# A decoder layer on one core: the first gate and up products in seven block products instead of eight

## The reference

```python
def swiglu(x, w_gate, w_up, w_down):
    return (jax.nn.silu(x @ w_gate) * (x @ w_up)) @ w_down
...
    x = x + 0.5 * swiglu(rmsnorm(x, ffn1_norm), ffn1_w_gate, ffn1_w_up, ffn1_w_down)
    h = rmsnorm(x, mix_norm)
    ...
    x = x + merged @ w_out
    x = x + 0.5 * swiglu(rmsnorm(x, ffn2_norm), ffn2_w_gate, ffn2_w_up, ffn2_w_down)
```

## Time and profile before

| | us |
|---|---|
| median of 3 runs (1655.89 to 1656.66) | 1655.98 |
| the profiled execution | 1656.42 |
| its span, first to last instruction | 1654.6 |
| TensorE busy in the span | 1609.5 |
| VectorE busy | 891.4 |
| ScalarE busy | 627.8 |

### The profile page before, as it was taken

The page is one execution under the profiler, slowest core; times in us unless marked ns, Lnnn a source line. Parts: engine busy times, 40 slices in busy tenths (PEclk is TensorE's granted clock), DMA queues, the critical chain, the costliest instruction groups (busy, mean ns, idle before and its releaser), DMA issues.

```text
span 1654.6 us, 30254 instructions
## 1 busy us (share of the span) xinstructions
PE 1609.5 (97%) x12544; PEld 1526.1 (92%) x12544; DVE 891.4 (54%) x1410; ACT 627.8 (38%) x993; POOL 4.5 (0%) x20
## 2 busy tenths in 40 slices
PE   7999999999999989999999999999999999999997
...
GB/s 128 92 80 89 89 77 93 97 82 85 68 114 56 126 269 71 64 82 84 103 91 100 92 125 102 109 224 92 87 88 90 98 103 96 99 93 105 85 79 67
DMA packets 246808, 164.34 MB, mean 99 GB/s; under 512 B 8350, under 2 KB 229779, under 8 KB 246714
## 3 DMA queue, kind: packets, MB, share of 16 engines
q1 hardware_dynamic: 246424, 162.46, 33.6%
...
q10 hardware_dynamic: 290, 0.57, 0.1%
...
## 4 chain that ended last, share of the span: by engine, by line
PE 88%; DVE 5%; ACT 2%; DMA 2%; issue 1%; SPq 1%; DVEq 0%; ACTq 0%
PE ps L444 57%; PE ps L1602 12%; PE ps L906 3%; PE ps L1125 2%; PE ps L1089 1%; PE ps L1325 1%; PE ps L1276 1%; PE ps L987 1%; PE ps L1395 1%; PE ps L427 1%; DVE small L2751 1%; PE ps L1174 1%; PE ps L1699 1%; PE ps L1439 1%; PE ps L1514 1%
## 5 line engine op out<-in xcount | busy, mean ns | idle before, releaser
L444 PE MATMUL ps<-xn_hi,w_hi 128*128 128x280 f32 (+1 forms) x1520 | 441.5, 290 | 3.6 <-DVE w_lo L415 2.9
L444 PE MATMUL ps<-xn_hi,w_lo 128*128 128x280 f32 (+1 forms) x1520 | 442.9, 291 | 0.0
L444 PE MATMUL ps<-xn_lo,w_hi 128*128 128x280 f32 (+1 forms) x1520 | 441.3, 290 | 0.0
L411 ACT ACTIVATE w_hi<-raw 128x1024 fp32r<-128x1024 f32 (+1 forms) x154 | 173.3, 1126 | 615.2 <-PE ps L444 602.8
L415 DVE TENSOR_TENSOR w_lo<-raw,w_hi 128x1024 fp32r<-128x1024 f32 (+1 forms) x154 | 201.3, 1308 | 181.9 <-ACT w_hi L411 181.7
L444 PEld LDWEIGHTS ps<-xn_hi,w_hi 128*128 128x128 f32 x1520 | 286.9, 189 | 4.5 <-DVE w_lo L415 3.1
L444 PEld LDWEIGHTS ps<-xn_hi,w_lo 128*128 128x128 f32 x1520 | 286.8, 189 | 0.0
L444 PEld LDWEIGHTS ps<-xn_lo,w_hi 128*128 128x128 f32 x1520 | 286.1, 188 | 0.0
L444 PE MATMUL ps<-h_hi,w_hi 128*128 128x280 f32 (+1 forms) x616 | 179.0, 291 | 0.0
L444 PE MATMUL ps<-h_hi,w_lo 128*128 128x280 f32 (+1 forms) x616 | 178.7, 290 | 0.0
L444 PE MATMUL ps<-h_lo,w_hi 128*128 128x280 f32 (+1 forms) x616 | 178.0, 289 | 0.0
...
## 6 DMA issues: line engine op xcount, KB each, us to landing
...
```

The lines of the kernel that those rows point to most:

```text
L411: act.activation(w_hi[s][:, 0:p.nk, :], raw[s][:, 0:p.nk, :], ACT.Copy).then_inc(hi_done[s], 1)
L444: mm = pe.matmul(ps[:, bank + half, 0:p.half], w[s][:, k, :], x[:, i, cols], start=first and k == 0 and a == 0, stop=last and k == p.nk - ...
```

## The change

The first gate and up stage becomes seven products as the second one is, at 280 columns. The functions of the second stage get the parameters `p` and `turn` (0 for the first, 1 for the second) and serve both; hardware loops of the first stage, and of the first down stage on TensorE, are written out. The blocks of the tokens are made as the tiles come from the transposes, pair by pair, with two buffers of `W4` and `T4` in the first stage; the token rows `xtok` and the buffers move to other places in memory. The sums of squares of the token rows move behind the blocks on ScalarE, and the row norm comes in panel 2, with bank 3 for that panel's first product. At the start the up panel is loaded ahead of the second half of the tokens. The first stage ends as the second does: all 22 tiles of h are rounded at the end, and `down_first` begins the down projection. In the second stage the rest of G of panel 1 moves ahead of the first gate sum. Semaphores are shared differently. The core of the diff, on SyncE, TensorE, ScalarE and VectorE in this order:

```diff
+        def a_bank(turn, j):
+            return 3 if turn == 0 and j == 2 else 4 * (j % 2)
...
+            def raw_gate(p, turn, j):
+                if j >= 1:
+                    after(sp, lo7, SPLIT7, turn, "g", j - 1)
...
-            load(sp, up1, 0, 0)
+            raw_gate(up1, 0, 0)
             load_x(0)
+            raw_up(up1, 0, 0)
             load_x(1)
-            load(sp, up1, 0, 1)
             sp.dma_start(con[:, 128:C_N], const_ap[:, 128:C_N]).then_inc(in_c, 16)
...
-            stream(up1, 1)
+            raw_panels(up1, 0)
             stream(down1)
...
-            def down(p, u):
-                down_tile(p, u, 0, 0, tiles=tile_lo)
-                down_tile(p, u, 0, 1)
...
+                down_first(p, u, 0)
+                for i in range(1, p.n):
+                    down_tile(p, u, i // 2, i % 2, at=place)
...
+            def seventh(p, w_of, block, bank, pairs=range(DT // 2), first=False):
+                for k in pairs:
+                    for a, (w, x) in enumerate(((0, XH), (0, XL), (1, XH))):
+                        mm = pe.matmul(ps[:, bank, 0:p.half], w_of(w)[:, k], x[:, k, block, 0:p.half],
+                                       start=first and k == 0 and a == 0, stop=k == DT // 2 - 1 and a == 2,
+                                       skip_group_check=True)
+                return mm
...
+            def fourth(p, turn, j):
+                after(pe, lo7, SPLIT7, turn, "u", j)
+                after(pe, part7, PART7, turn, "r3", j)
+                seventh(p, a22(j % 2), 5, a_bank(turn, j)).then_inc(product7, 1)
+            def third(p, turn, j):
+                after(pe, hidden7, HIDDEN7, turn, "u2", j)
+                seventh(p, s4(j % 2), 1, 4 * (j % 2) + 1).then_inc(product7, 1)
+            def sixth(p, turn, j):
+                after(pe, lo7, SPLIT7, turn, "s2", j)
+                after(pe, part7, PART7, turn, "r1", j)
+                seventh(p, s2, 6, a_bank(turn, j)).then_inc(product7, 1)
+            def seventh_last(p, turn, j):
+                after(pe, part7, PART7, turn, "r2", j)
+                seventh(p, s3, 4, a_bank(turn, j)).then_inc(product7, 1)
+            def strassen(p, turn):
+                if turn:
+                    after(pe, lo7, SPLIT7, turn, "g", 0)
+                    for k in range(DT // 2 - 1):
+                        token(turn, "l3", k)
+                        early_12(p, k)
+                    after(pe, lo7, SPLIT7, turn, "s31", 0)
+                    for k in range(DT // 2 - 1):
+                        token(turn, "lt", k)
+                        seventh(p, s1, 3, 1, (k,), first=True)
+                end_12(p, turn)
+                token(turn, "lq", DT // 2 - 1)
+                sixth(p, turn, 0)
+                if turn:
+                    norm(2, p, (3, 7))
+                seventh_last(p, turn, 0)
+                for j in range(1, FT):
+                    c = 4 * (j % 2)
+                    if j == 2 and turn == 0:
+                        row_norm()
+                    after(pe, lo7, SPLIT7, turn, "g", j)
+                    if j >= 2 and a_bank(turn, j) == c:
+                        after(pe, hidden7, HIDDEN7, turn, "h1", j - 2)
+                    seventh(p, a11, 0, a_bank(turn, j), first=True).then_inc(product7, 1)
+                    if j >= 2:
+                        after(pe, gate7, GATE7, turn, "g1", j - 2)
+                    if j == 2 and turn == 0:
+                        pe.wait_ge(rn_ready, 1)
+                    seventh(p, a12, 2, c + 2, first=True).then_inc(product7, 1)
+                    fourth(p, turn, j - 1)
+                    after(pe, lo7, SPLIT7, turn, "s31", j)
+                    if j >= 2:
+                        after(pe, gate7, GATE7, turn, "g2", j - 2)
+                    seventh(p, s1, 3, c + 1, first=True)
+                    sixth(p, turn, j)
+                    third(p, turn, j - 1)
+                    seventh_last(p, turn, j)
+                fourth(p, turn, FT - 1)
+                third(p, turn, FT - 1)
...
-            for i in range(DT + 1):
+            for i in range(DT):
                 keep_warm(IDLE.get(i, 0))
-                for s, ks in EARLY.get(i, ()):
-                    first_product(pe, up1, 0, s, ks)
-                if i == DT:
-                    break
                 for c in range(2):
                     if 128 * i == X_CHUNKS[c][0]:
                         pe.wait_ge(in_x[c], 16 * 5)
@@ -1039,28 +1192,34 @@
                     mm = transpose(ps[:, 4 + 2 * (i % 2) + c0 // 512, c0 % 512:c0 % 512 + 112],
                                    xtok[:, t, 128 * i:128 * i + 128], 112)
                 mm.then_inc(xt_full, 1)
+                if i == DT - 3:
+                    after(pe, lo7, SPLIT7, 0, "g", 0)
+                    token(0, "l3", 0)
+                    early_12(up1, 0)
+            token(0, "l3", 1)
+            early_12(up1, 1)
+            after(pe, lo7, SPLIT7, 0, "s31", 0)
+            for k in range(2):
+                token(0, "lt", k)
+                seventh(up1, s1, 3, 1, (k,), first=True)
+            early_12(up1, 2)
+            token(0, "lt", 2)
+            seventh(up1, s1, 3, 1, (2,), first=True)
             x_done(pe, DT - 2)
             x_done(pe, DT - 1)
-            pe.wait_ge(dg_ready, 1)
-            for t in range(5):
-                c0 = 64 + 112 * t
-                mm = pe.matmul(ps[:, 4 + c0 // 512, c0 % 512:c0 % 512 + 112], ones[0:112, :], dg[:, t, :],
-                               start=True, stop=True)
-            mm.then_inc(nm_full, 1)
-            first_product(pe, up1, 0, 1, [DT - 2, DT - 1])
-            up(up1)
+            strassen(up1, 0)
             down(down1, up1)
...
+            g_split(0, 0)
             act.wait_ge(ring_dve, 1)
             x_copy(1)
-            hi(0)
-            hi(1)
+            scaled_first(0)
+            scaled_first(1)
+            blocks_hi(up1, 0, 0)
             x_copy(3)
-            hi(2)
-            hi(3)
-            square_rows(0)
-            hi(4)
-            split_hi(act, up1, 0, 1)
-            hi(5)
-            square_rows(1)
-            square_rows(2)
-            hi(6)
-            hi(7)
+            scaled_first(2)
+            scaled_first(3)
+            differences_hi(up1, 0, 0)
+            blocks_hi(up1, 0, 1)
+            x_copy(5)
+            scaled_first(4)
+            scaled_first(5)
+            s31_split(0, 0)
+            differences_hi(up1, 0, 1)
+            x_copy(6)
+            blocks_hi(up1, 0, 2)
+            x_copy(7)
+            scaled_first(6)
+            scaled_first(7)
+            differences_hi(up1, 0, 2)
+            blocks_hi(up1, 0, 3)
+            differences_hi(up1, 0, 3)
+            s2_split(0, 0)
+            u_split(0, 0)
+            for t in range(3):
+                square_rows(t)
+            first_sum(up1, 0, 0)
+            g_split(0, 1)
             square_rows(3)
+            second_sum(up1, 0, 0)
+            s2_split(0, 1)
             square_rows(4)
+            u_split(0, 1)
+            third_sum(up1, 0, 0)
+            s31_split(0, 1)
+            first_sum(up1, 0, 1)
             act.wait_ge(in_c, 16)
             act.wait_ge(ss_ready, 5)
-            act.activation(r0[:, 0:5], r0[:, 0:5], ACT.Ln, bias=con[0:112, C_EPS:C_EPS + 1], scale=1.0 / D).then_inc(rn_log, 1)
-            act.wait_ge(rn_log, 1)
-            act.activation(r0[:, 0:5], r0[:, 0:5], ACT.Exp, scale=-0.5).then_inc(r0_ready, 1)
-            act.wait_ge(nm_full, 1)
-            copy(rn[:, :], x_tile(0)).then_inc(rn_ready, 1)
-            gated(up1, ACT.Silu, h_hi)
+            row_rms()
+            panels_of(up1, 0, down1)
...
+            g_rest(0, 0)
+            differences(up1, 0, 0)
+            blocks_rest(up1, 0, 0)
+            differences(up1, 0, 1)
+            differences_rest(up1, 0, 0)
+            blocks_rest(up1, 0, 1)
+            sums_31(0, 0)
+            sum_2(0, 0)
+            sum_4(0, 0)
+            differences(up1, 0, 2)
+            differences_rest(up1, 0, 1)
+            blocks_rest(up1, 0, 2)
+            s31_rest(0, 0)
+            differences(up1, 0, 3)
+            differences_rest(up1, 0, 2)
+            blocks_rest(up1, 0, 3)
+            differences_rest(up1, 0, 3)
+            s2_rest(0, 0)
...
+            def differences(p, turn, k):
+                n, w4, t4 = p.half, W4s[turn][k % 2], T4s[turn][k % 2]
+                after(v, token_hi, TOKEN_HI, turn, "w", 2 * k + 1)
+                if k >= 2 - turn:
+                    after(v, token_lo, TOKEN_LO, turn, "lq", k - 2 + turn)
+                link(v.tensor_tensor(t4[:, 0:2, 0:n], w4[:, 1:3, 0:n], w4[:, 0:1, 0:n].to_broadcast([128, 2, n]), ALU.subtract))
+                link(v.tensor_tensor(t4[:, 3, 0:n], t4[:, 0, 0:n], w4[:, 2, 0:n], ALU.add))
+                v.tensor_tensor(t4[:, 2, 0:n], t4[:, 3, 0:n], w4[:, 3, 0:n], ALU.subtract).then_inc(token_lo, 1)
...
+            def panels_of(p, turn, down_):
```

(45 more changed lines are left out.)

875 lines of the change are left out of this document (407 added, 468 removed).

## The result

| | before | after |
|---|---|---|
| median of 5 runs each, same chip (us) | 1655.98 (1654.86 to 1657.31) | 1639.09 (1638.56 to 1645.71) |
| profiled execution (us) | 1656.42, span 1654.6 | 1639.09, span 1637.3 |
| ratio after / before | | 0.9906, 95% interval 0.9887 to 0.9926 |

By the medians the kernel became 16.9 us faster, where 19.0 had been forecast: 1639.1 against 1637.0, inside the range and inside the forecast's own bounds. The interval of the ratio, which is taken over all runs and so differs a little from the quotient of the medians, means 12 to 19 us. The page of after, TensorE's busy time and the chain by engine, answers to the earlier trace rows: 264 matmuls fewer, VectorE 126 us more, and VectorE's share of the chain that ended last grew from 5% to 7%.

A forecast was written before the change was run, and what follows sets the result against it. TensorE, busy 97% of the span, was taken as the bound. Down projection start: 44.0 + 230.1 (1788 matmuls) + 2.9 + 2.5 + 0.9 = 280.4 against 299.42, 19.0 us less: 1656.0 to 1637.0; range 1630 to 1646, own bounds 1633 to 1641.

The forecast's parts named there:

- term 4: End of first gate and up stage: TensorE waits 0.58 us (third sum) and 1.89 us (h_lo), 2.5 us in all.
- Term 1: Matmuls of a panel: 84 instead of 96 at 0.1287 us, 10.81 instead of 12.32 us, saving 31.7 us over 21 panels.
- Term 2: Start, by ScalarE and VectorE queues: panel 0's seventh product ends at 44.0; panel 1 began at 39.05 before, 4.95 us lost.
- Term 3: Gaps behind the start: 0.45 us third sum, 1.2 us S31 of panel 1, 1.2 us norm matmuls; 2.9 us.
- first down matmul at 280: Profile sign: the first down projection matmul (h_hi) starts at 280 +- 4 us, against 299.42 before.
- Term 5: Clock at the start: 1.2 GHz level in two stretches, one under waits, one under panel 0's sixth and seventh products; about 0.9 us.
- The third sign: Stages behind the first: the prediction is wrong if they shift by more than 1 us.
- (a): Rival: start nearly hidden, seventh product ends at 40.5, 2.9 us of gaps covered; 25.4 us less, 1630.6; chance 0.13.
- (b): Rival: start costs more, three half-clock stretches at 1.7 us and 2 us of order waits; 12 us less, 1644; chance 0.24.
- (c): Rival: VectorE becomes the bound in first-stage panels; partial 11.1 us, 1643, chance 0.04; full 12.0 us, 1662, chance 0.02.

The follow-up runs named there:

- e_squares: Changed kernel with two rows of squares instead of three ahead of the first sum on ScalarE, one moved behind the second sum: 1641.86 us, one run.
- e_both: Changed kernel with one row of squares fewer ahead of the first sum and three more h tiles rounded ahead of the last gate: 1635.82 us, 0.9880 of before.
- e_hold: e_both with 23 filler matmuls in TensorE's longest idle time of the start and 5 ahead of panel 0's sixth product: 1635.65 us, 0.9868 of before.
- e_dve5x_swap: Changed kernel with five extra VectorE operations a panel from panel 4, and ScalarE's third-sum copy ahead of the previous panel's gate: 1652.09 us, one run.
- e_tokens_first: Changed kernel with the second half of the tokens loaded ahead of the up panel, as before the change: 1642.40 us, one run.

## Why the prediction was right, and which steps failed

The sum had the first down matmul at 280.4, which is +266.3 from copy 1; it came at +264.97. Of the 280.4, 1.9 us are a wait that falls behind that matmul (term 4); without it the sum says +264.4, 0.6 us too early. The terms one by one:

**Term 1, the matmul.** 0.1287 us was taken between 0.1283 and 0.1290, 0.1292 was measured. The upper end, the second stage's own row scaled with the columns, was the right one; the first stage's 0.1283 belongs to another stream of matmuls. Over 1788 matmuls that is 0.9 us. The panels themselves became 12.32 - 10.85 = 1.47 us shorter each: at the row's 0.1283 us the 12 matmuls removed are worth 1.54, and the 84 that stay take 0.0009 us more each.
By the Trainium skill (TensorE: Matmul & The Clock Gate, Back-to-back issue gap) the gap of one isolated matmul of 280 columns would be 119.2 ns, an estimate by its formula. The window of after shows 129.2 ns, so the trace does not agree for this stream, and the row was the better price.

**Term 2, the start.** The layout of both queues put the wait ahead of S31's rest until 32.1 (measured 30.62 with copy 1 1.64 us earlier, so 32.26 on its scale), the sixth product at +25.8 from copy 1 (measured +26.28) and named both releasers. Of the 0.5 us, 0.06 lie ahead of the squares, 0.13 between ScalarE's copy and the product, and 0.29 are one mis-sized price: three rows of squares took 3.41 us instead of 3 x 1.04. The price was right for before, readout included (ScalarE of before; the next row of squares starts at 24.39, 1.04 us behind this one):

```profile
23.35 1.04 ACT L1829 ACTIVATE junk<-xtok 112x1024 f32<-112x1024 f32 x1
24.30 0.18 ACT L1829 ACTIVATION_READ_ACCUMULATOR junk<-xtok 112x1 f32 x1
```

What the layout missed is in the change itself: all rows of squares now write one buffer, so each waits until the one before is done.

```diff
-                act.activation(junk[:, t, :], xtok[:, t, :], ACT.Square, accum_out=r0[:, t:t + 1]).then_inc(ss_ready, 1)
...
+                    act.wait_ge(ss_ready, t)
+                act.activation(junk[:, :], xtok[:, t, :], ACT.Square, accum_out=r0[:, t:t + 1]).then_inc(ss_ready, 1)
```

In after a row with such a wait behind it takes 1.17 and 1.19 us, the one in front of the copy, which does not wait for it, 1.05. In e_squares, with one such wait less, it is 1.16 and 1.06.

**Term 3, the gaps behind the start.** 2.9 us were put down (0.45 for the third sum, 1.2 for S31, 1.2 for the norm's ten matmuls). The first did not show, of the second 0.25 us did, and the matmuls took 1.04. From P1 to D there are 233.5 us, and 1788 x 0.1292 + 1.04 + 0.58 for the third sum at the end make 232.6; the other 0.9 are those 0.25 and pauses of 0.1 to 0.2 us around the norm, the third sum and the first down matmul. The S31 gap is real, but appears in full only where TensorE is ahead: 0.87 us in e_both and e_hold (and 0.25 for the third sum in e_both). In after the half clock until 43.6 had made TensorE late, so that it hardly sees it. The prediction added up the clock and this gap; of two delays that run side by side only the longer one shows.

**Table loads.** No drain showed; ScalarE of after:

```profile
47.31 1.28 ACT L1886 ACT_TABLE_LOAD   x1
48.61 0.30 ACT L1886 ACTIVATE small<-small,con 112x5 f32<-112x5 f32 x1
```

The Trainium skill (ScalarE: Activation LUTs, What ACT_TABLE_LOAD costs) adds a drain to each switch; here the next operation starts 0.02 us behind the load, as in the earlier trace rows, and nothing is to be added.

**Term 4, the end.** The waits are 0.58 and 1.86 us, as read from the earlier trace rows. Two things were wrong. The second lies inside the down stage, eight microseconds behind its first matmul, not before it, so the sign "first down matmul at 280" was 1.9 us late by construction, while the sum to the end was not. And the term that failed: the half clock from 285.9 to 289.3 behind that wait, 1.5 us of the 3.75 by which the down stage grew; 1.86 are the wait and 0.4 lie around it. VectorE of after, the rests that TensorE waits for:

```profile
283.43 1.63 DVE L424 TENSOR_TENSOR w_lo<-raw,w_hi 128x1408 fp32r<-128x1408 f32 x1 [0.82 <-ACT w_hi L420]
284.97 9.22 DVE L2539 TENSOR_TENSOR h_lo<-h,h_hi 128x560 fp32r<-128x560 f32 x14
```

They stand behind a rest of w_lo that itself waited 0.82 us. In the second stage of before the wait of 1.89 us had full clock behind it, so its row did not show this price; the earlier trace rows, half clock behind a wait of 2.90, did, and the prediction used it for the start alone. It is the largest miss: +3.75 us for the down stage instead of +1.9. Not every execution has it (138.0 in five of the kernels above).

**Term 5, the clock at the start.** Two stretches were expected and came, one under waits and one under the sixth and seventh product. The size was 0.9 us; from p6 to P1 it is 1.25 us in after (5.18 against the 3.94 of e_dve5x_swap, with the full clock) and 1.35 in e_squares, and at most 0.15 at D, except in e_tokens_first, where with ten microseconds of it D came 2.2 us later.

**The sum again.** Against the forecast saving of 19.0 us of span: +0.7 for P1 (0.5 ahead of the sixth product, most of it the squares, and 0.2 of clock), +0.9 for term 1, -1.0 for term 3, +1.85 in the down stage (1.5 clock, 0.35 around the wait), +0.9 for the stages behind, which vary that much by themselves, and -1.64 because the tokens came earlier. Together 1.7, so 17.3. That the total is so near is in part luck: two terms cancel, and the 1.64 are chance, as copy 1 lies anywhere from 12.48 to 15.46 in the kernels here. Without the 1.64 the span would have shrunk by 15.7 us.

**Its own signs.** Panels took 10.85 us, not above 11, and the seventh product of panel 0 ended at 43.9, not beyond 47. The third sign did show: the stages behind were not to shift by more than 1 us, and the down stage grew by 1.85 us more than the wait foreseen in it, half clock for the most part. The path and the releasers were as forecast; the price of a wait behind which the clock falls was not.

**The rivals.** (a) would have needed ScalarE's queue 3.5 us shorter than laid out; e_squares shows that this queue is the bound, and it was laid out too short by 0.4. Of its other half, the covered gaps, 1.0 of 2.9 us came true. (b) had the wrong price: the half-clock stretches came, but those of the start hardly moved D, since ScalarE and VectorE set it, and only the one in the down stage showed. Its order waits did not come: 0.5 us instead of 2. Its 7 us also held the 0.9 of clock that the sum had counted already. (c) did not occur, but its condition was nearer than written: the prediction took VectorE's busy time of the second stage (9.5 of 10.81, cover 1.3), where the first stage's queue is 10.07 long. The break-even of 11.7 us a panel is bracketed: at 12.36 the kernel is slower than before, at 11.53 (1652.09, one run, against 1656.92) it is still faster.

**What stays open.** What places the half clock in an execution is not known from these runs; kernels with the same start have it in different places, and one has none there. Whether the order of the loads in e_tokens_first has a part in its ten microseconds is open. e_both's gain in device time lies within the intervals.
